# A two-layer streaming encoder step: early gathered rows summed by ScalarE and GpSimd, and another order of the first expert scores

## What is computed

```python
def one_block(xb):                       # xb (tokens, 1024)
    q = (xb @ w_q).reshape(blk, PEER_HEADS, 2, D_HALF)          # 8 heads, two halves
    sc = jnp.einsum('thpd,hpnd->thpn', q, sub_keys)             # 128 keys each
    top_s, top_i = lax.top_k(sc, 16)
    cand_s = top_s[:, :, 0, :, None] + top_s[:, :, 1, None, :]
    best_s, sel = lax.top_k(cand_s.reshape(...), 16)            # 16 of 16384 experts
    gate = jax.nn.softmax(best_s, axis=-1)
    act = jax.nn.gelu(jnp.einsum('thkd,td->thk', exp_u[idx], xb))
    w = gate * act
    return jnp.einsum('thk,thkd->td', w, exp_v[idx])
```

## Time and profile before

| what | us |
|---|---|
| median of 3 runs | 3265.97 (3261.54 to 3266.31) |
| the profiled execution | 3254.12 |
| its span | 3252.3 |
| choices and first scores, layer 0 | 436 to 503 |
| first 17 builds, layer 0 | 503 to 610 |
| pairs, layer 0 | 610 to 1568 |
| attention of group d, layer 1 | 1897 to 1962 |
| choices and first scores, layer 1 | 2074 to 2168 |
| first 17 builds, layer 1 | 2168 to 2275 |
| pairs, layer 1 | 2275 to 3223 |

### The profile page before, as it was taken

How to read it: one execution, slowest core, us unless ns; L and a number is a source line. 1 busy time by engine, 2 the same in 40 slices (tenths; PEclk the granted TensorE clock), 3 DMA queues, 4 the chain that set the end, 5 groups by cost and what they waited for, 6 DMA issues and landing times.

```text
span 3252.3 us, 46708 instructions
## 1 busy us (share of the span) xinstructions
PE 2958.9 (91%) x17310; PEld 2582.9 (79%) x17310; DVE 2473.6 (76%) x5433; ACT 811.2 (25%) x2388; POOL 1056.1 (32%) x840
## 2 busy tenths in 40 slices
PE   6898989999999999967878978789999999999876
PEld 6797778888888888855666957678888888888755
DVE  2366799988888888877533776898888888888876
ACT  4332222212111111211354362222112111112111
POOL 4532122333333333333354321122333323333331
PEclk8999999999999999988877968889999999999988
DMA  5336778999999999999311257678999999999995
GB/s 163 96 97 246 262 273 322 360 421 422 422 422 420 415 416 421 407 422 416 131 58 52 97 194 266 229 262 311 420 421 422 422 422 418 419 417 417 406 421 200
DMA packets 159967, 1042.99 MB, mean 321 GB/s; under 512 B 18480, under 2 KB 23920, under 8 KB 44096
## 3 DMA queue, kind: packets, MB, share of 16 engines
q0 software_dynamic: 92160, 671.13, 50.8%
q1 hardware_dynamic: 63648, 357.59, 28.5%
q10 hardware_dynamic: 4000, 12.36, 1.1%
HBM read 1033.28 MB, written 7.86 MB: 320 GB/s over the span
## 4 chain that ended last, share of the span: by engine, by line
PE 40%; DMA 40%; DVE 11%; issue 7%; POOL 1%; ACT 1%; SPq 0%; DVEq 0%; ACTq 0%; POOLq 0%
DMA gata<-uvg,idxg 24%; DMA gatb<-uvg,idxg 15%; PE bank L713 11%; PE bank L516 8%; DVE acc L1600 5%; PE bank L726 4%; PE bank L503 3%; PE bank L700 3%; PE bank L505 3%; PE bank L504 3%; PE bank L602 1%; PE bank L533 1%; PE bank L860 1%; DVE gata L1592 1%; PE bank L838 1%
## 5 line engine op out<-in xcount | busy, mean ns | idle before, releaser
L726 PE MATMUL bank<-a,V 128*128 128x256 f32 x4096 | 947.8, 392 | 102.5 <-DVE a L1583 102.5
L726 PEld LDWEIGHTS bank<-a,V 128*128 128x128 f32 x4096 | 805.3, 197 | 229.0 <-issue 112.6
L713 PE MATMUL bank<-xd,U 128*128 128x256 f32 x4096 | 940.2, 389 | 0.0
L1273 POOL DMA_INDIRECT gata<-uvg,idxg x428 | 525.9, 1229 | 1236.2 <-DVE acc L1600 1176.8
L713 PEld LDWEIGHTS bank<-xd,U 128*128 128x128 f32 x4096 | 790.3, 195 | 107.7 <-issue 0.2
L1592 DVE CUSTOM_DVE_ANT_0 gata<-gata,xrow 128x1024 f32<-128x1024 f32 x428 | 522.9, 1222 | 201.7 <-DMA gata<-uvg,idxg 194.9
L1600 DVE SCALAR_TENSOR_TENSOR acc<-gata,wgt,acc 128x1024 f32<-128x1024 f32 x428 | 548.5, 1281 | 32.6 <-ACT wgt L1085 32.5
L1083 ACT ACTIVATE act<-dot 128x1 f32<-128x1 f32 x640 | 129.3, 202 | 1489.3 <-DVE dot L1592 1489.2
L1273 POOL DMA_INDIRECT gatb<-uvg,idxg x212 | 254.0, 1198 | 551.1 <-DVE acc L1600 541.9
L1592 DVE CUSTOM_DVE_ANT_0 gatb<-gatb,xrow 128x1024 f32<-128x1024 f32 x212 | 259.1, 1222 | 106.6 <-DMA gatb<-uvg,idxg 105.3
L700 PEld LDWEIGHTS bank<-B,oneA 128*128 128x128 f16 x4096 | 280.0, 150 | 18.4 <-issue 6.4
(11 more groups left out here) (193 smaller groups left out, 2516.7 us busy)
## 6 DMA issues: line engine op xcount, KB each, us to landing
U<-uvd SPq DMA_DIRECT2D x128, 1024.0 KB
V<-uvd SPq DMA_DIRECT2D x128, 1024.0 KB
raw<-lin SPq DMA_DIRECT2D x152, 512.0 KB, 3.5
gata<-uvg,idxg POOLq DMA_INDIRECT x428
hsp<-h ACTq DMA_DIRECT2D x2, 2304.0 KB, 12.4
hx<-hsp SPq DMA_DIRECT2D x2, 2304.0 KB, 16.6
gatb<-uvg,idxg POOLq DMA_INDIRECT x212
sk_g<-skT ACTq DMA_DIRECT2D x2, 1024.0 KB, 4.8
```

What stands on the lines that cost most here:

```text
L713: mm = pe.matmul(bank[s][:, TD * t:TD * t + TD], U[:, s, o:o + P], xd[:, k, :], start=(t == 0 and k == 0), stop=(k == DT - 1), skip_group_ ...
L726: mm = pe.matmul(bank[b][:, TD * (d % 2):TD * (d % 2) + TD], V[:, s, o:o + P], a[:, s, TD * k:TD * k + TD], start=(first and k == 0 and d ...
L1273: pool.indirect_dma_start(row(l, s), None, uvg[l], bass.IndirectOffsetOnAxis(idxg[:, s:s + 1], 0)).then_inc(g_in[s % SLOTS], 16)
```

## The change

- Steps that stand at places ahead of `hot` (all but the hot ones; `SIDE` is their number) are summed in another way: ScalarE, after the two small instructions, multiplies the v half of the row by the weight in place (128 x 1024), and GpSimd adds it to `acc`. VectorE keeps their `dot_x` alone. GpSimd's add of step s stands right ahead of its gather of step s + 6.
- The early steps are 56 in layer 0 (34 of them summed by GpSimd) and 59 in layer 1 (37): `mix` 1 to 2, `mid2` 2 to 3, `sel3` 3 to 4, `sel4` 3 to 5; in layer 1 `sel2` 2 to 3, `sel3` 3 to 4, `sel4` 3 to 5.
- ScalarE's weights of most places stand later: those of `add` and `att` one place on, those of `mid` one head on, those of `mix` in the next loop, those of `sel2` and `sel3` behind the first gelu of the next choice, and those of `sel4` behind the two instructions that need both turns (`gates_high`).
- The ring starts at another place and four small arrays of the choice move, so that eight scores can be made during the choices. Layer 0: 3, 1, 2, 1 scores around its two ranks (before 2, 1, 2, 1 and one more behind). Layer 1: 3, 1, 1, 1, 1, 1 around three ranks (before 1, 1, 1, 1, 1, 1 and one more behind), so that 8 in place of 9 scores are left for the first builds.

```diff
--- before.py
+++ after.py
-RING_AT = 10
+RING_AT = 8
 BUSY = 9
-FIRST = (2, 1)
+FIRST = ({3: 3, 4: 2}, {2: 3, 3: 1, 4: 1})
...
 AT = (
-    [("mid1", 3), ("two", 3), ("mix", 1), *[(f"add{m}", 1) for m in range(6)], ("mid2", 2), *[(f"top{m}", 1) for m in range(8, HP)],
-     ("sel3", 3), ("sel4", 3), *[(f"hot{m}", 1 + (m % 4 == 0)) for m in range(LEAD)]],
+    [("mid1", 3), ("two", 3), ("mix", 2), *[(f"add{m}", 1) for m in range(6)], ("mid2", 3),
+     *[(f"top{m}", 1) for m in range(8, HP)], ("sel3", 4), ("sel4", 5), *[(f"hot{m}", 1 + (m % 4 == 0)) for m in range(LEAD)]],
     [*[(f"att{n}", 1) for n in range(1, 16, 2)], *[(f"add{m}", 1) for m in range(6)], ("mid1", 3),
      *[(f"top{m}", 1) for m in range(8, HP)],
-     ("sel2", 2), ("sel3", 3), ("sel4", 3), *[(f"hot{m}", 1 + (m % 4 == 0)) for m in range(LEAD)]])
+     ("sel2", 3), ("sel3", 4), ("sel4", 5), *[(f"hot{m}", 1 + (m % 4 == 0)) for m in range(LEAD)]])
 EARLY = tuple(sum(n for _, n in a) for a in AT)
+SIDE = tuple(sum(n for p, n in a if p[:3] != "hot") for a in AT)
...
-        cand, cr = arena(PH, NC), arena(PH, NC)
+        cand, cr = (at_(n, 87040 + 1600 * i, [P, PH, NC], F32) for i, n in enumerate(("cand", "cr")))
...
-        sm, rs = arena(PH), arena(PH)
+        sm, rs = (at_(n, 90240 + 32 * i, [P, PH], F32) for i, n in enumerate(("sm", "rs")))
...
                 for i in range(2 if l else 3, NTC):
-                    for k in range(FIRST[l]):
+                    for k in range(FIRST[l][i]):
                         expert_scores(l, n + k, (n + k) % 2)
...
                 for i in range(n, RING0 - 1):
                     expert_scores(l, i, i % 2)
+                n = max(n, RING0 - 1)
                 for m in range(LEAD):
                     build(l, m, m % 2)
-                    if m % 2 == 0:
-                        expert_scores(l, RING0 - 1 + m // 2, (RING0 - 1 + m // 2) % 2)
+                    if m % 2 == 0 and n + m // 2 < RING:
+                        expert_scores(l, n + m // 2, (n + m // 2) % 2)
...
-                        weights_at(int(norm[1] == "4"), f"add{m}")
+                        weights_at(int(norm[1] == "4"), f"add{m - 1}" if m else "mix")
...
-                        if m == 12:
+                        if m == 13:
                             weights_at(0, "mid1")
+                        if m == 2 * DT - 1:
                             weights_at(0, "two")
...
-                    weights_at(0, "mix")
                     squares_of_h("n2d", "outd")
...
                         if m == 2:
                             gate_exp(l, mid)
+                        if m == 3:
                             weights_at(l, f"mid{mid}")
...
                 act.activation(wgt[:, k:k + 1], act8[:, k:k + 1], ACT.Copy, scale=gateg[:, s:s + 1])\
                     .then_inc(wgt_done, 1)
+                if s < SIDE[l]:
+                    v = row(l, s)[:, D:RD]
+                    act.wait_ge(wgt_done, NSTEP * l + s + 1)
+                    act.activation(v, v, ACT.Copy, scale=wgt[:, k:k + 1]).then_inc(vw_done, 1)

             def experts(l):
                 n = 0
                 for i in range(2 if l else 3, NTC):
-                    for k in range(FIRST[l]):
+                    for k in range(FIRST[l][i]):
                         gelu(l, n + k)
-                    n += FIRST[l]
+                        if k == 0:
+                            weights_at(l, f"sel{i - 1}")
+                    n += FIRST[l][i]
                     gate_exp(l, i)
                     gelu(l, n)
-                    weights_at(l, f"sel{i}")
                     n += 1
                 for c in DC:
                     gates_high(l, c)
-                gelu(l, n)
+                weights_at(l, f"sel{NTC - 1}")
+                for i in range(n, RING0 - 1):
+                    gelu(l, i)
+                n = max(n, RING0 - 1)
                 weights_at(l, "hot0")
-                for i in range(n + 1, RING0 - 1):
-                    gelu(l, i)
...
-                        weights_at(1, f"att{n}")
+                        weights_at(1, f"att{n - 1}")
...
+            def axpy(l, s):
+
+                n = min(s // P, 2)
+                pool.wait_ge(vw_done, SIDE[0] * l + s + 1)
+                if s == 0:
+                    pool.wait_ge(acc_zero, l + 1)
+                pool.wait_ge(ax_done, NSTEP * l + s)
+                pool.tensor_tensor(acc[:, n, :], acc[:, n, :], row(l, s)[:, D:RD], ALU.add).then_inc(ax_done, 1)
+
             def experts(l):
...
                 for s in range(SLOTS, NSTEP):
+                    if s - SLOTS < SIDE[l]:
+                        axpy(l, s - SLOTS)
                     if s % P == 0:
...
             def gathered(l, s):

                 dot_x(l, s)
-                if s == 0:
-                    dve.wait_ge(acc_zero, l + 1)
-                else:
+                if s > SIDE[l]:
                     axpy(l, s - 1)
```

7 lines of the change are left out of this document (4 added, 3 removed).

## The result

The changed kernel took 3280.32 us (median of 6 runs, 3278.56 to 3290.59), the kernel before 3263.85 us beside it (6 runs): a ratio of 1.0067, 95% interval 1.0046 to 1.0089. The forecast was a ratio of 0.997. The profiled execution after has a span of 3276.9 us, 24.6 us more than before.

The account below looks back on a forecast made before the run. Three limits: DMA in the pairs, TensorE in the first builds, VectorE with ScalarE close behind in early places. Layer 0's -1.5 and layer 1's -8.2 gave -9.7 us on 3265.97: 3256; 8-in-10 range 3232 to 3284.

Parts of the forecast that it names:

- layer 0 to the first scores: Gated MLP +4 us from holds and a late row, head 4 +4.8 from later weights; first scores at 444.8.
- first scores to first build, layer 0: Choices of layer 0: TensorE's 10.5 us wait filled, rows for sel4 land late; first build at 512.4, +9.2 in all.
- tail, layer 0: Last 14 pairs of layer 0: five rows fewer to transfer, 2.5 us each, -12.5 us.
- attention d: Layer 1's attention of group d: ScalarE's product makes it the bound, 7.93 against 7.2 us in eight pairs of units, +5.8.
- choices, layer 1: Layer 1's last choice: row 36 waits for the third sel3 sum, its dot ending at 2167.3 against 2164.26, +3 us.
- ring: Layer 1's first builds, TensorE-bound: eight scores made by then, not seven, so one of 7.0 us fewer, -7 us.
- tail, layer 1: Tail pairs of layer 1: four rows fewer to transfer, -10 us.
- The rival that they would not shorten: Tails: their end is set by something the DMA share hides, so -22.5 us falls away; 3279 us, chance 0.06.
- the third at t0 + 23.4: Layer 0's choices: row 33, third behind sel3's weights, lands 23.4 us after t0; sel4 ends at t0 + 24.6 = 508.3.
- t0: Layer 0's choices: the gelu at 483.7 us, when the four weights of sel3 were forecast to begin.
- about six new holds: GpSimd's new sums holding up VectorE's two-input instructions, each costing 0 to 2.4 us; about six counted.
- if 20 more fall where VectorE sets the pace: Port rival: 20 more holds by GpSimd's sums at half a sum each, +24 us, so 3280; chance 0.24.

Follow-up runs that it names:

- b_rows: Kernel before with the changed kernel's 56 and 59 early steps alone, all sums on VectorE: 3257.43 us, ratio 0.9988.
- a_old_counts: Changed kernel with the 51 and 55 early steps of the kernel before, all else as in the change: 3280.37 us, ratio 1.0075.
- a_fill: Changed kernel with each of GpSimd's 71 sums replaced by a fill of acc with zeros, about as long: 3265.95 us, ratio 1.0023.
- c_att: Kernel before with ScalarE's product and GpSimd's sum only for the eight steps of layer 1's attention of group d: 3262.36 us, ratio 1.0013.
- c_top: Kernel before with ScalarE's product and GpSimd's sum only behind the searches of heads 8 to 15: 3248.12 us, 0.9969; measured again 3253.36, 0.9974.

## Why the prediction was wrong, point by point

| term | forecast | measured in the two profiles |
|---|---|---|
| layer 0 to the first scores | +8.8 | +15.2 |
| first scores to first build, layer 0 | +0.4 | +7.6 |
| row 35, first builds | +2 | +4.2 |
| tail, layer 0 | -12.5 | -15.3 |
| attention d | +5.8 | +10.4 |
| choices, layer 1 | +3 | +7.9 |
| ring | -7 | -4.6 in the builds, +6.9 in the pairs |
| tail, layer 1 | -10 | -12.9 |
| the rest | 0 | +5.2 |

Forecast were -9.7 us in sum, and the two profiles differ by +24.6. Of the 34 us between, 21 lie ahead of layer 0's first scores, in the choices of both layers and in layer 0's first builds, 9 in the ring, 5 in the attention and 5 in the rest; the tails gave 6 back. The step that failed is the price of the early steps ahead of the pairs; the points below take it apart.

- **The tails were right**, in place and nearly in size (2.5 us a row forecast, 3.1 and 3.2 measured). The rival that they would not shorten fell. That it is the row's transfer that comes back is not shown by the size: VectorE's dot and sum of a row are 2.5 us too. For the transfer speaks the DMA share of 1.0, where VectorE is busy for 129 of 165 us.
- **What the rows cost in the choices had no term.** I priced an extra early step at what ScalarE and GpSimd add. b_rows has no product and no sum of theirs and yet pays 5.0 and 10.8 us from the first scores to the first builds, and 8.3 up to layer 0's first scores. In the changed kernel itself the old counts (a_old_counts) take 6.4 and 11.8 off the same two stretches. I had nothing for a fourth and fifth step on VectorE in front of `take` and the first gate block.
- **The step "the third at t0 + 23.4" failed.** It made row 33's landing set the end of `sel4`. After the change no dot of `sel4` waits for a DMA; VectorE reaches the first of them only at 509.59, 17.5 us later than before. The moment that the forecast calls t0 came at 494.66, 11 us late, 6.9 of them there at the first score already (451.67 against 444.8). That `sel4` then ended at 519.51, 24.9 us behind t0 where I had 24.6, is luck: held masks and dots fill this time, and not a landing. With fills a wait for row 33 does appear, 3.69 us, and its landing takes 515.90 - 506.76 = 9.1 us, not the 12.2 that I took from the pairs, where the DMAs are full. That TensorE would stand idle ahead of the first build was right; the idle time of 8 us that I wanted to see on the dots was not there.
- **The count of holds failed.** I had counted about six new holds that matter. There are 48 more lengthened instructions than before, by 80 us in sum. My rival named this ("if 20 more fall where VectorE sets the pace") and gave 3280, which is the measured time; that the number fits is luck, since the runs do not bear it out as the one mechanism. The lock is worth at least 14 us (a_fill), the rest of the sum, its length in the chain above all, 29, ScalarE's product 13, the later places some 11, each with an error of several us; and against them stand the 36 us that VectorE's relief gave.
- **"The searches have one input, and I take nothing for them" was right for the searches, not for every one-input instruction.** The attention's multiplication by 1/sum (L1739) was held five times, for 1.7 to 2.1 us.
- **In the gated MLP** I had two holds on the norms of group d; two came, 2.77 us each, and a third on `xd` at 372.8. At head 4 the 6 us were right (6.42). The first scores came 15.2 us late in place of 8.8. The extra rows are not what made it: the old counts take 2.6 us off this stretch, while with the same rows and neither product nor sum, and none of VectorE's sums, it takes 161.8 us, less than before. The lock makes 8.7 us of it (fills, 169.1), where I had 4 for the gated MLP with all its holds, and none behind it.
- **The attention's 5.8 us was right in size for product and sum at the old places** (c_att 5.7), which is luck in part: the term was ScalarE's product alone, with ScalarE as the bound. In the changed kernel ScalarE is busy for 62.97 us, as forecast (8 x 7.9), but the stretch takes 78.2; product and sum each alone leave 73.4 and 73.6, neither 68.0. The change also puts the weights one unit later, worth another 4 to 7 us; I had read that line of the diff and given it nothing.
- **The ring's 7 us failed** for a reason that my first paragraph had stated: from 650 us on the DMAs are full. If my reading above holds, what is won ahead of a stretch bound by the DMAs is won only if transfers start sooner as well. I subtracted it beside the tail's rows, which do take bytes away. The layer 0 delay came through the pairs whole (+27.6 at pair 0, +28.2 at pair 48), the ring's gain did not.

No kernel here beats both by much. c_top does by 0.3%: 3248 and 3253 us in two measurements.

## What to carry to other kernels

Work taken off a busy engine is not gone when it goes to GpSimd: ask which instructions of VectorE run beside it, what it now delays (here the next gather, by 2.4 us a row), and whether the longer chain still fits in the slack. Here the relief was worth 36 us and the moved work cost 58. Price a moved step both where it leaves and where it arrives, with the work that it always had (b_rows) and not only with what the change adds to it. Try such a change place by place: the same edit gave -9 us behind the searches and +7 us in the choices, and together with the other edits 13 us that none of them had alone.

## What the runs showed of the hardware

**Fills hold some VectorE instructions too.** A fill of GpSimd reads nothing, and masks and dots in the choices ran beside it at their own length. The one-input multiplication over 128 x 128 in the attention did not, and neither did two one-input casts over 128 x 128 in the choices (1.33 us in place of 0.26). VectorE in the choices and in the attention, run with fills; the two instructions of L1739 take 0.5 to 0.7 us undisturbed:

```profile
465.48 1.33 DVE L1507 CAST W<-bp 128x128 f16<-128x128 uint32 x1
...
1931.62 2.71 DVE L1739 TENSOR_SCALAR S_d<-S_d,rin 128x128 f32<-128x128 f32 x2
1932.01 2.31 DVE L1613 CUSTOM_DVE_ANT_0 gata<-gata,xrow 128x1024 f32<-128x1024 f32 x1
```

The dot behind it starts late as well. The Trainium skill (SBUF — State Buffer, Who interferes with whom) counts `tensor_scalar` among the operations that can take the ports shared with GpSimd; the trace agrees, with 2.2 us (2.51 for one of the two). So a_fill leaves part of the lock in, and its 14 us are a lower bound for it.

**Two values of the start.** TensorE's granted clock between 100 and 130 us was 0.83 in some profiled executions and 0.56 to 0.60 in the others, with the same instructions there. Windows of the kernel after and of c_top:

```profile
100.00:130.00 30.00, 24.14 (x126) 18.31 (x125) 17.28 (x39) 9.90 (x17) 12.33 (x10) 0.83 0.15 45
```

```profile
100.00:130.00 30.00, 24.61 (x92) 18.57 (x93) 20.06 (x37) 7.68 (x15) 9.46 (x9) 0.60 0.14 42
```

In all 20 traces 0.83 goes with a first gather at 272 to 274 us and 0.56 to 0.60 with one at 277 to 281. From 78 to 100 us the clock is 1.00 (2.4 GHz) in all that I looked at, with TensorE busy for 21 to 22 of the 22 us. Then come gaps; TensorE is busy for 24 of 30 us in either case, but in the second, where it is mostly granted 1.2 GHz, 92 matmuls are done and not 126. The number of instructions of each engine ahead of the first gather is the same in all of them. It makes some 6 us, as much as most effects looked for here. Each kernel has one trace, so that it changes between executions of one kernel is not shown directly; but the eight executions with 0.83 lie 0.3 to 10.4 us under the median of their kernel, and of the twelve others none is more than 0.8 under and one is 10.4 over.
